# Token tiles in plain column order, and gather loads that read every fourth column

## The chip, the cores and the metric

The kernel runs on one core of one Trainium2 chip. The metric is device time in microseconds (us) of one execution; the median of three runs stands for the kernel, and lower is better. One execution was also profiled, and every row below comes from it.

## What is computed

Two transformer-like blocks run one after the other on 256 tokens of width 1024. The first has two layers of gated linear attention with spatial gating, cross attention and a mixture of experts; the second has block attention, a state space mixer, another mixture of experts and a gated projection. So there are three mixtures of experts (called 0, 1 and 2 below), and the change touches only these. Each has 16 experts with a hidden width of 512 and takes two experts for a token:

```python
for e in range(N_EXPERTS):
    h = jax.nn.silu(xt @ w_gate[e]) * (xt @ w_up[e])
    y = y + gate[:, e:e + 1] * (h @ w_down[e])
```

`gate` is zero but for the two experts that a token's router chose. Data are float32 all through.

## The kernel before, in words

**An expert works on its own tokens.** When no expert has more than 64 of the 256 tokens, each expert gets a tile of 64 columns that holds its tokens only, with the model's 1024 values in 8 chunks of 128 partitions (`own_even` for one quad of four experts, `own_odd` for the next). Moving the tokens into those columns is a matrix product, `gather` (line 966): the stationary operand is a 128 x 128 piece of `x_tok` (tokens on partitions, 128 model columns), and the moving operand is `picked` (tokens on partitions, 4 experts x 64 places, 256 columns), which has a one where a token takes a place. `x_tok` is a pair, a value rounded for the multiplier (`aux_high`) and the rest (`aux_low`), and there are two tiles of 128 tokens, so one chunk takes four matmuls, and one call of `gather`, for two chunks, takes eight, each with a load of its own.

**Where the gathers stand.** TensorE (PE) makes four calls for the first quad right after routing (`experts`, line 952; 32 matmuls). The other three quads are gathered inside the loop over experts of `experts_own` (line 1041), one call per expert for the first twelve experts, between the sum of an earlier expert's output (`add`, line 1103) and the up projection (`gate_up`, line 1055); that is 12 x 8 = 96 matmuls. ScalarE (ACT) then copies each result from PSUM into `own_even` or `own_odd` (`packed`, line 1507).

**Column order.** The expert weights come in by DMA with four consecutive rows on one partition (`"(p r) n -> p (r n)"` for each half of the matrix). So chunk c of the activations must hold, on partition p, the model column 512 (c // 4) + 4 p + (c % 4). Before the change the token tiles are stored in that order already: ScalarE's line 1569 (in `routing_input`) and VectorE's line 2005 (in `routing_input_low`) read plain columns and write each value 128 places after its neighbour, and `gather` then loads 128 adjacent columns.

**Order around routing.** ScalarE goes, for each of the two token tiles, through `tiles_high` (line 1454, the transposed activations for the router), line 1569, and line 1570 (the residual). VectorE (DVE) goes through `tiles_low` (line 1802) and line 2005 for each tile, and then the router's small steps, up to `choose` (line 1996), which makes `picked`. TensorE's router product (lines 935, 936, 940, 949) needs lines 1454 and 1802 of both tiles; the gathers need line 2005 of both and `picked`. SyncE's queue of weight loads waits for line 2005 once per mixture, before it lends `x_res` to the weights (line 415).

The branch for crowded experts (`experts_all`) also reads `x_tok`; the profiled execution has no row of it.

Of the kernel before, what the change touches and what calls it, by code (L numbers as in the profile page):

```python
# [18 lines left out]
F32 = mybir.dt.float32  # L19
F32R = mybir.dt.float32r  # L20
ACT = mybir.ActivationFunctionType
ALU = mybir.AluOpType
AX = mybir.AxisListType.X

P = 128
# [24 lines left out]
def build(nc, a, out):  # L50
    DEPTH, D = a["w_in"].shape[0], a["w_in"].shape[1]
    T = a["x"].shape[1]
# [92 lines left out]
    OWN = P // 2  # L145
    QUAD = 4
# [131 lines left out]
    with ExitStack() as ctx:  # L278
# [34 lines left out]
        ident = sb("ident", [P, P])  # L313
# [31 lines left out]
        S = {n: sem(n) for n in names}  # L345
# [144 lines left out]
        all_hid = own[1][:, 0:FC, :].rearrange("p c n -> p (c n)").rearrange("p (t n) -> p t n", t=TT)  # L490
        all_hidT = own[1][:, FC:2 * FC, :]

        def regrouped(v):

            return v.rearrange("q (i r p) -> q i p r", i=2, r=4)

        def runs(v):

            return v.rearrange("q (i p r) -> q i p r", i=2, r=4)

        x_tok = [v[:].rearrange("p c t -> p (c t)").rearrange("p (t n) -> p t n", t=TT) for v in (aux_high, aux_low)]
        gates = st[:, 512:512 + TT * NE].rearrange("p (t n) -> p t n", t=TT)
# [206 lines left out]
        def _(pe):  # L709
# [256 lines left out]
            def gather(m, q, g, dst):  # L966

                for c in range(2):
                    for part in range(2):
                        for t in range(TT):  # L970
                            c0 = (2 * g + c) * P
                            i = pe.matmul(dst[:, c * QUAD * OWN:(c + 1) * QUAD * OWN], x_tok[part][:, t, c0:c0 + P],  # L972
                                          picked[q % 2][:, t, :, 0, :], start=(part + t == 0), stop=(part + t == TT))
                i.then_inc(x_filled[m], 1)

# [13 lines left out]
            def experts_all(m):  # L989

                G, U, TS, Y0 = (ps[:, 2 * s:2 * s + 2, :] for s in (G_SLOT, U_SLOT, T_SLOT, Y0_SLOT))
                residual(m, start=False, stop=True)
                pe.wait_ge(x_packed[m], GROUPS)
                flat = ps[:, 0:4, :].rearrange("p b n -> p (b n)")
                for c in range(KC):
                    for t in range(TT):
                        for part in range(2):
                            i = pe.matmul(flat[:, c * T + t * P:c * T + t * P + P], x_tok[part][:, t, c * P:c * P + P].bitcast(F32), ident[:],
                                          start=(part == 0), stop=(part == 1))
                i.then_inc(tokens_turned[m], 1)  # L1000
                pe.wait_ge(tokens_copied[m], 2)

                def wide(e, part):
                    if e:
                        pe.wait_ge((silu_done, hid_ready)[part][m], e)
                    for j in range(2):
                        w = tile(m, (gate_at, up_at)[part](e) + j)
                        for r in range(4):
                            c = 4 * j + r
                            for t in range(TT):  # L1010
                                i = pe.matmul((G, U)[part][:, t, :], tok_T[:, c, t * P:t * P + P], w[:, FF * r:FF * r + FF], start=(c == 0), stop=(c == KC - 1))
                        i.then_inc(tiles_used, 1)

                for part in range(2):
                    wide(0, part)
                for e in range(NE):
                    pe.wait_ge(hid_ready[m], e + 1)
                    if e:
                        pe.wait_ge(y_added[m], TT * e)
                    dst = TS.rearrange("p b n -> p (b n)").rearrange("p (c t) -> p c t", t=T)  # L1020
                    by_run = all_hid.rearrange("p t (i s r) -> p t i r s", i=2, r=2)
                    for i2 in range(2):
                        for r in range(2):
                            for t in range(TT):
                                i = pe.transpose(dst[:, 2 * i2 + r, t * P:t * P + P], by_run[:, t, i2, r, :], ident[:])
                    i.then_inc(hid_turned[m], 1)
                    if e + 1 < NE:
                        for part in range(2):
                            wide(e + 1, part)
                    pe.wait_ge(hid_copied[m], e + 1)  # L1030
                    for j in range(2):
                        w = tile(m, down_at(e) + j)
                        for r in range(2):
                            for t in range(TT):
                                for b in range(2):
                                    i = pe.matmul((Y0, TS)[t][:, b, :], all_hidT[:, 2 * j + r, t * P:t * P + P], w[:, D * r + 512 * b:D * r + 512 * b + 512],
                                                  start=(j + r == 0), stop=(j + r == 2))
                        i.then_inc(tiles_used, 1)
                pe.wait_ge(y_added[m], TT * NE)
# [116 lines left out]
            for l in range(DEPTH):  # L1156
# [16 lines left out]
                for t in range(TT):  # L1173
                    i = pe.matmul(slot_ps(L + "z")[:, t * DQK:t * DQK + DQK], aT[:, t * P:t * P + P], w_a2, start=True, stop=True)
# [7 lines left out]
                for g in range(SG):  # L1182
                    i = pe.transpose(slot_ps(L + "wsT")[:, g * P:g * P + P], ws_raw[:, g, :], ident[:])
# [6 lines left out]
                for k in range(PAIRS):  # L1190
                    for t in range(TT):
                        i = pe.matmul(slot_banks(L + "decay")[:, 1, 4 * k + 2 * t:4 * k + 2 * t + 2], log_a[:, t, k * P:k * P + P], half[:], start=True, stop=True)
# [4 lines left out]
                for k in range(PAIRS):  # L1197
                    for t in range(TT):
                        i = pe.transpose(slot_ps(L + "qT")[:, k * T + t * P:k * T + t * P + P], qk[:, t, k * P:k * P + P], ident[:])
# [11 lines left out]
                for k in range(PAIRS):  # L1211
                    begin(L + f"kv{k}")
                    for c in range(NCH):
                        t, hf = c // 2, c % 2
                        rows = slice(LCH * hf, LCH * hf + LCH)
                        i = pe.matmul(slot_banks(L + f"kv{k}")[:, hf, 256 * t:256 * t + 256], k_dec[rows, t, k * P:k * P + P],
                                      v_gla[rows, t, k * 2 * DV:(k + 1) * 2 * DV], start=True, stop=True)
# [6 lines left out]
                for t in range(TT):  # L1224
                    for g in range(SG):
                        i = pe.matmul(slot_banks(L + "mix_sgu")[:, t, g * P:g * P + P], wsT[:, g, :], gelu_v[:, t, g * P:g * P + P], start=True, stop=True)
# [3 lines left out]
                for t in range(TT):  # L1230
                    begin(L + f"o{t}")
                    for k in range(PAIRS):
                        for par in range(2):
                            rows = slice(DK * par, DK * par + DK)
                            for hf in range(2):
                                c = 2 * t + hf
                                i = pe.matmul(slot_banks(L + f"o{t}")[LCH * hf:LCH * hf + LCH, par, k * P:k * P + P],
                                              qT_gla[rows, k, c * LCH:c * LCH + LCH], state[rows, k, c, :], start=True, stop=True)
# [24 lines left out]
                for t in range(TT):  # L1263
                    begin(L + f"pT{t}")
                    pe.wait_ge(S["p_ready"], TT * l + t + 1)
                    for h in range(XH):
                        for b in range(TT):
                            i = pe.transpose(slot_ps(L + f"pT{t}")[:, (2 * h + b) * P:(2 * h + b + 1) * P], prob[:, t, h, b * P:b * P + P], ident[:])
                    full(i, L + f"pT{t}")
                operand_ready(L + "pT0", L + "pT1", L + "xva", L + "xvb")  # L1270
                for k in range(2):
                    begin(L + f"oT{k}")
                    for f in range(4):
                        fb = 4 * k + f
                        for b in range(TT):
                            i = pe.matmul(slot_ps(L + f"oT{k}")[:, f * T:f * T + T], xv[:, b, fb * P:fb * P + P], pT[:, fb // 2, b, :],
                                          start=(b == 0), stop=(b == TT - 1))
# [145 lines left out]
        def _(act):  # L1423
            chain = Counter(act, S["act_chain"])
            n, limit = 0, moe_at[0][0]
            A = nc.scalar.activation
# [138 lines left out]
            def routing_input(names, src, scale):  # L1565

                for t in range(TT):
                    tiles_high(act_high, names[t:t + 1], t)
                    A(regrouped(x_tok[0][:, t, :]), runs(src[:, t, :]), ACT.Copy).then_inc(S["tok_high"], 1)
                    A(y_acc[:, t, :], x[:, t, :], ACT.Copy, scale=scale).then_inc(S["residual_ready"], 1)  # L1570

            for l in range(DEPTH):
# [55 lines left out]
                for t in range(TT):  # L1628
                    act.wait_ge(S["smax_ready"], TT * l + t + 1)
                    for h in range(XH):  # L1630
                        i = A(prob[:, t, h, :], slot_ps(L + f"s{t}")[:, h * T:h * T + T], ACT.Exp, bias=neg_max[:, t, h:h + 1],
                              scale=float(XD) ** -0.5, accum_out=p_sum[:, t, h:h + 1])
# [92 lines left out]
            for t in range(TT):  # L1725
                act.wait_ge(S["u_ready"], t + 1)
                for g in range(SGR):
                    i = A(usq[:, t, g * 512:g * 512 + 512], zs[:, t, g * 512:g * 512 + 512], ACT.Square, accum_out=u_ms[:, t, g:g + 1])
# [39 lines left out]
        def _(dve):  # L1768
            V = nc.vector
# [159 lines left out]
            flat = lambda v: v.rearrange("p t g e -> p t (g e)")  # L1929
# [70 lines left out]
            def routing_input_low(names, src, m):  # L2000

                for t in range(TT):
                    tiles_low(act_low, act_high, names[t:t + 1], t)
                    dve.wait_ge(S["tok_high"], TT * m + t + 1)
                    V.tensor_tensor(regrouped(x_tok[1][:, t, :]), runs(src[:, t, :]), regrouped(x_tok[0][:, t, :]).bitcast(F32), ALU.subtract).then_inc(S["tok_low"], 1)

            def experts(m):

# [92 lines left out]
            for l in range(DEPTH):  # L2101
# [28 lines left out]
                for t in range(TT):  # L2130
                    for g in range(SG):
                        i = V.bn_stats(v_bn[:, t, g, :], gelu_v[:, t, g * P:g * P + P])
                link(i)
                for t in range(TT):
                    for g in range(SG):
                        i = V.bn_aggr(v_mv[:, t, g, :], v_bn[:, t, g, :])
# [3 lines left out]
                for t in range(TT):  # L2140
                    for g in range(SG):
                        at = slice(g * P, g * P + P)
                        i = V.scalar_tensor_tensor(gelu_v[:, t, at], gelu_v[:, t, at], v_mv[:, t, g, 0:1], sln_g[:, at], ALU.subtract, ALU.mult)
# [291 lines left out]
```

## Time and profile before

| | us |
|---|---|
| median of the three runs | 1481.27 |
| lowest and highest run | 1480.82, 1482.7 |
| the profiled execution's own time | 1480.01 |
| its span, first to last instruction | 1478.3 |
| TensorE busy in the span | 1396.9 |
| VectorE, ScalarE busy | 607.5, 498.2 |

The mean granted TensorE clock is 0.982 of full speed. The span is 1.7 us shorter than the same execution's own time. Matmuls overlap their neighbours: the duration of one is its way through the array, and the distance between two starts (called the pitch below) is what one costs in a stream. "PEld" is the load of a stationary operand, which overlaps the matmul ahead of it.

### The profile page before, as it was taken

To read this page: it belongs to the slowest core of one execution; us is meant where nothing else is said; L and a number is where in the kernel's file an instruction comes from. 1 tells how busy PE (TensorE), PEld (TensorE's weight loads), DVE (VectorE), ACT (ScalarE), POOL (GpSimd) and SP (SyncE) were. 2 spreads that over 40 slices of the span, in tenths; PEclk is the share of its full clock that TensorE was granted. 3 is DMA by queue.
4 is the path that set the end of the run, shared out by engine and by line. 5 is a ranking of instruction groups with operands and counts; after the bars stand their busy time and mean duration, and the time that the engine had idled before them with its cause. 6 is when DMAs were issued, how large, how long until landed. Compare 5 with 4: busy or idle time off the path is not lost.

```text
span 1478.3 us, 20927 instructions
## 1 busy us (share of the span) xinstructions
PE 1396.9 (94%) x8927; PEld 1000.5 (68%) x8927; DVE 607.5 (41%) x1001; ACT 498.2 (34%) x695; POOL 53.8 (4%) x95
## 2 busy tenths in 40 slices
PE   7999998999997999998999999799999989999977
PEld 5788976555554788986655554788787765555546
DVE  4677435111114585646111111657766561111124
ACT  5454434111113544443211111466565331111123
POOL 5000000000001000000000000000000000000000
PEclk9999999999999999999999999999999999999989
DMA  9556458999999455647899999453443769999970
GB/s 326 198 166 205 148 212 327 423 421 421 421 420 343 139 170 171 206 168 311 331 420 421 421 420 410 172 171 115 142 143 129 280 248 412 421 421 420 421 294 29
DMA packets 90807, 422.71 MB, mean 286 GB/s; under 512 B 7068, under 2 KB 7232, under 8 KB 53840
## 3 DMA queue, kind: packets, MB, share of 16 engines
q1 hardware_dynamic: 86528, 407.92, 70.8%
q0 software_dynamic: 4176, 13.30, 2.6%
q8 instruction: 78, 1.28, 0.4%
q14 instruction: 25, 0.20, 0.0%
HBM read 420.15 MB, written 1.05 MB: 285 GB/s over the span
## 4 chain that ended last, share of the span: by engine, by line
PE 88%; DVE 5%; ACT 4%; issue 2%; POOL 0%; DMA 0%; DVEq 0%; POOLq 0%; ACTq 0%
PE ps L1055 23%; PE ps L1091 12%; PE ps L753 5%; PE ps L754 5%; PE ps L758 5%; PE ps L972 4%; PE ps L1103 4%; PE ps L867 3%; PE ps L801 3%; PE ps L874 3%; PE ps L868 3%; PE ps L802 3%; PE ps L806 3%; PE ps L1080 1%; PE ps L914 1%
## 5 line engine op out<-in xcount | busy, mean ns | idle before, releaser
L1782 DVE TENSOR_TENSOR raw_low<-raw,w_high 128x1024 fp32r<-128x1024 f32 x198 | 237.4, 1223 | 171.2 <-ACT w_high L1440 170.5
L1440 ACT ACTIVATE w_high<-raw 128x1024 fp32r<-128x1024 f32 x198 | 206.6, 1058 | 258.6 <-PE ps L758 115.2
L2067 DVE TENSOR_TENSOR hid<-silu_g,ps 128x256 f32<-128x256 f32 x48 | 29.6, 616 | 259.8 <-PE ps L1055 259.8
L753 PE MATMUL ps<-w_high,act_high 128*128 128x512 f32 x272 | 110.6, 407 | 6.4 <-DVE raw_low L1782 3.6
L2075 DVE SCALAR_TENSOR_TENSOR out_low<-ps,stats,out_high 128x512 fp32r<-128x512 f32 x48 | 36.1, 751 | 182.3 <-ACT out_high L1546 182.3
L754 PE MATMUL ps<-raw_low,act_high 128*128 128x512 f32 x272 | 108.4, 399 | 0.0
L758 PE MATMUL ps<-w_high,act_low 128*128 128x512 f32 x272 | 103.3, 393 | 0.0
L1055 PE MATMUL ps<-raw,own_odd 128*64 128x256 f32 x800 | 91.6, 380 | 0.0
L1546 ACT ACTIVATE out_high<-ps,stats 128x512 fp32r<-128x512 f32 x48 | 33.0, 687 | 161.5 <-PE ps L1091 161.5
L867 PE MATMUL ps<-act_high,w_high 128*128 128x256 f32 x288 | 81.7, 287 | 5.4 <-issue 3.4
L1541 ACT ACTIVATE spread<-ps 128x288 fp32r<-128x288 f32 x48 | 19.7, 411 | 186.7 <-PE ps L1080 186.7
L1055 PEld LDWEIGHTS ps<-raw,own_odd 128*64 128x64 f32 x800 | 56.6, 137 | 36.8 <-issue 11.0
L868 PE MATMUL ps<-act_high,raw_low 128*128 128x256 f32 x288 | 81.2, 285 | 0.0
L874 PE MATMUL ps<-act_low,w_high 128*128 128x256 f32 x288 | 78.4, 285 | 0.0
L1091 PE MATMUL ps<-raw,hT 128*64 128x512 f32 x328 | 76.2, 599 | 0.0
L801 PE MATMUL ps<-w_high,act_high 128*128 128x512 f32 x192 | 75.2, 392 | 0.0
L802 PE MATMUL ps<-raw_low,act_high 128*128 128x512 f32 x192 | 74.8, 389 | 0.0
L1055 PE MATMUL ps<-raw,own_even 128*64 128x256 f32 x640 | 74.6, 382 | 0.0
L753 PEld LDWEIGHTS ps<-w_high,act_high 128*128 128x128 f32 x272 | 52.7, 194 | 20.9 <-issue 6.8
L659 POOL TENSOR_TENSOR stats<-stats,exponent 128x1 f32<-128x1 f32 (+2 forms) x24 | 19.9, 830 | 1217.7 <-DVE stats L1851 302.1
L1537 ACT ACTIVATE silu_g<-ps 128x256 f32<-128x256 f32 x48 | 18.4, 384 | 130.7 <-PE ps L1055 130.7
L2071 DVE COPY hT<-ps 128x256 f32<-128x256 f32 x48 | 20.4, 425 | 102.1 <-PE ps L1067 102.1
(411 smaller groups left out, 2570.8 us busy)
## 6 DMA issues: line engine op xcount, KB each, us to landing
raw<-in_w_up SPq DMA_DIRECT2D x46, 1024.0 KB, 11.3
raw<-in_w_in SPq DMA_DIRECT2D x44, 1024.0 KB, 9.2
raw<-in_w_gate SPq DMA_DIRECT2D x44, 1024.0 KB, 13.1
raw<-in_w_down SPq DMA_DIRECT2D x41, 1024.0 KB, 16.7
work<-in_w_down SPq DMA_DIRECT2D x23, 1024.0 KB, 19.7
work<-in_w_gate SPq DMA_DIRECT2D x21, 1024.0 KB, 7.9
w_lent<-in_w_gate SPq DMA_DIRECT2D x18, 1024.0 KB, 13.0
w_lent<-in_w_down SPq DMA_DIRECT2D x14, 1024.0 KB, 14.8
```

Source lines behind the costliest of these rows:

```text
L753: pe.matmul(bank[:, t, :], xh, wh, start=(k == 0), stop=False)
L754: pe.matmul(bank[:, t, :], xh, wl, start=False, stop=False)
L758: return pe.matmul(bank[:, t, :], src[1][:, k, t * P:t * P + P], weights(n, 512 * c, 512 * c + 512)[0], start=False, stop=(k == KC - 1))
L801: pe.matmul(slot_banks(names[t])[:, b, :], xh, wh, start=(k == 0), stop=False)
L802: pe.matmul(slot_banks(names[t])[:, b, :], xh, wl, start=False, stop=False)
L867: pe.matmul(bank, wh, src[0][:, k, 0:T], start=(k == 0), stop=False)
L868: pe.matmul(bank, wl, src[0][:, k, 0:T], start=False, stop=False)
L874: return pe.matmul(bank, wh, src[1][:, k, 0:T], start=False, stop=(k == KC - 1))
L1055: i = pe.matmul((G, U)[part][OWN * h:OWN * h + OWN, 0:256], own[e // QUAD % 2][:, c, OWN * (e % QUAD):OWN * (e % QUAD) + OWN], w[:, FF * r ...
L1091: i = pe.matmul(Y[OWN * h:OWN * h + OWN, :], hT[:, r, OWN * j:OWN * j + OWN], w[:, D * r + 512 * h:D * r + 512 * h + 512], start=(j + r == ...
L1440: A(split_unit(n)[0], raw_unit(n), ACT.Copy).then_inc(high_ready, 1)
L1782: V.tensor_tensor(split_unit(n)[1], raw_unit(n), split_unit(n)[0].bitcast(F32), ALU.subtract).then_inc(low_ready, 1)
```

## The change

The token tiles are now written in plain column order, by both engines. The gather picks its columns itself: chunk c is read as columns 512 (c // 4) + (c % 4), and then every fourth one, 128 in all, so two neighbours in the stationary operand lie 16 bytes apart in memory. The number, the shapes and the order of the instructions are the same on every engine; only the way in which two kinds of store and two kinds of load step through memory differs.

```diff
@@ -490,13 +490,9 @@
         all_hid = own[1][:, 0:FC, :].rearrange("p c n -> p (c n)").rearrange("p (t n) -> p t n", t=TT)
         all_hidT = own[1][:, FC:2 * FC, :]
 
-        def regrouped(v):
-
-            return v.rearrange("q (i r p) -> q i p r", i=2, r=4)
-
-        def runs(v):
-
-            return v.rearrange("q (i p r) -> q i p r", i=2, r=4)
+        def columns_of(v, c):
+
+            return v.rearrange("q (i p r) -> q i r p", i=2, r=4)[:, c // 4, c % 4, :]
 
         x_tok = [v[:].rearrange("p c t -> p (c t)").rearrange("p (t n) -> p t n", t=TT) for v in (aux_high, aux_low)]
         gates = st[:, 512:512 + TT * NE].rearrange("p (t n) -> p t n", t=TT)
@@ -968,8 +964,7 @@
                 for c in range(2):
                     for part in range(2):
                         for t in range(TT):
-                            c0 = (2 * g + c) * P
-                            i = pe.matmul(dst[:, c * QUAD * OWN:(c + 1) * QUAD * OWN], x_tok[part][:, t, c0:c0 + P],
+                            i = pe.matmul(dst[:, c * QUAD * OWN:(c + 1) * QUAD * OWN], columns_of(x_tok[part][:, t, :], 2 * g + c),
                                           picked[q % 2][:, t, :, 0, :], start=(part + t == 0), stop=(part + t == TT))
                 i.then_inc(x_filled[m], 1)
 
@@ -995,7 +990,7 @@
                 for c in range(KC):
                     for t in range(TT):
                         for part in range(2):
-                            i = pe.matmul(flat[:, c * T + t * P:c * T + t * P + P], x_tok[part][:, t, c * P:c * P + P].bitcast(F32), ident[:],
+                            i = pe.matmul(flat[:, c * T + t * P:c * T + t * P + P], columns_of(x_tok[part][:, t, :], c).bitcast(F32), ident[:],
                                           start=(part == 0), stop=(part == 1))
                 i.then_inc(tokens_turned[m], 1)
                 pe.wait_ge(tokens_copied[m], 2)
@@ -1566,7 +1561,7 @@
 
                 for t in range(TT):
                     tiles_high(act_high, names[t:t + 1], t)
-                    A(regrouped(x_tok[0][:, t, :]), runs(src[:, t, :]), ACT.Copy).then_inc(S["tok_high"], 1)
+                    A(x_tok[0][:, t, :], src[:, t, :], ACT.Copy).then_inc(S["tok_high"], 1)
                     A(y_acc[:, t, :], x[:, t, :], ACT.Copy, scale=scale).then_inc(S["residual_ready"], 1)
 
             for l in range(DEPTH):
@@ -2002,7 +1997,7 @@
                 for t in range(TT):
                     tiles_low(act_low, act_high, names[t:t + 1], t)
                     dve.wait_ge(S["tok_high"], TT * m + t + 1)
-                    V.tensor_tensor(regrouped(x_tok[1][:, t, :]), runs(src[:, t, :]), regrouped(x_tok[0][:, t, :]).bitcast(F32), ALU.subtract).then_inc(S["tok_low"], 1)
+                    V.tensor_tensor(x_tok[1][:, t, :], src[:, t, :], x_tok[0][:, t, :].bitcast(F32), ALU.subtract).then_inc(S["tok_low"], 1)
 
             def experts(m):
 
```

## Rows read from the trace of the kernel before

**Rows 1.** Page: span, busy share of each engine; then time granted and DMA in three mixtures

```profile
span 1478.3 us, 20927 instructions
PE 1396.9 (94%) x8927; PEld 1000.5 (68%) x8927; DVE 607.5 (41%) x1001; ACT 498.2 (34%) x695; POOL 53.8 (4%) x95
...
core 0: us, PE busy (x) PEld busy (x) DVE busy (x) ACT busy (x) POOL busy (x), PEclk, DMA share, GB/s
240.00:470.00 230.00, 221.20 (x1600) 125.04 (x1600) 41.71 (x90) 40.80 (x74) 0.56 (x1) 0.99 0.99 403
```

**Rows 2.** Chain of waits, one expert of mixture 0: start us, us, what

```profile
300.05 1.15 PE ps L972 x8
301.20 3.60 PE ps L1055 x32
304.81 0.46 PE ps L1080 x2
305.26 3.58 PE ps L1091 x16
308.85 3.45 PE ps L1055 x32
312.30 0.37 PE ps L1067 x2
312.67 1.12 PE ps L1103 x8
313.79 1.14 PE ps L972 x8
```

**Rows 3.** Waits of PE and of SyncE's queue: us in total, times, longest us

```profile
PE ps L972 <- DVE picked_even L1996: 5.8, 3, 1.9
...
PE ps L914 <- DMA x_res<-in_x: 4.6, 1, 4.6
...
SPq L597 <- PE ps L1055: 404.0, 175, 14.4
...
SPq L415 <- DVE aux_low L2005: 15.0, 2, 9.3
```

**Rows 4.** The gather's line alone, by stretch: opening and loop of each mixture (PE, PEld)

```profile
240.00:247.00 7.00, 5.56 (x32) 5.38 (x32) 0.76 0.47 193
247.00:430.00 183.00, 14.56 (x96) 12.12 (x96) 1.00 1.00 412
...
701.00:708.00 7.00, 5.55 (x32) 5.38 (x32) 0.76 0.51 215
...
1209.00:1213.30 4.30, 4.06 (x32) 3.89 (x32) 1.00 0.01 4
1213.30:1400.00 186.70, 14.57 (x96) 12.13 (x96) 1.00 1.00 411
```

**Rows 5.** The gather's line: duration ns min/median/max; then its timeline, low and full clock

```profile
L972 PEld LDWEIGHTS ps<-picked_even,aux_high x96: 186/189/336, 240.7 to 1308.8; 128*128 128x128 f32 x96
...
242.33 0.63 PE L972 MATMUL ps<-picked_even,aux_high 128*128 128x256 f32 x2
242.76 0.63 PE L972 MATMUL ps<-picked_even,aux_low 128*128 128x256 f32 x2
...
300.56 0.40 PE L972 MATMUL ps<-picked_even,aux_high 128*128 128x256 f32 x2
300.80 0.40 PE L972 MATMUL ps<-picked_even,aux_low 128*128 128x256 f32 x2
```

**Rows 6.** Timeline: six loads of 128 columns with matmuls of 16 columns

```profile
237.49 0.74 PEld L1146 LDWEIGHTS ps<-stats,tri 128*128 128x128 f32 x6 [1.48 <-issue]
```

**Rows 7.** ACT and DVE, stores out of order and plain: duration ns min/median/max

```profile
L1569 ACT ACTIVATE aux_high<-x_res x4: 2019/2092/2188, 225.6 to 690.5; 128x1024 fp32r<-128x1024 f32 x4
...
L1570 ACT ACTIVATE work<-x_res x6: 1057/1064/1141, 227.4 to 1198.9; 128x1024 f32<-128x1024 f32 x6
...
L2005 DVE TENSOR_TENSOR aux_low<-x_res,aux_high x4: 1985/2014/2083, 228.0 to 692.7; 128x1024 fp32r<-128x1024 f32 x4
...
L1782 DVE TENSOR_TENSOR raw_low<-raw,w_high x198: 1214/1225/1228, 10.5 to 1454.4; 128x1024 fp32r<-128x1024 f32 x198
```

**Rows 8.** Timeline around routing, mixture 0, and VectorE's first router step of mixture 2

```profile
227.01 1.09 PE L914 MATMUL ps<-ident,x_res 128*128 128x128 f32 x8 [0.68 <-DVE x_res L1840]
...
228.33 1.02 ACT L1454 ACTIVATE act_high<-ps 128x1024 fp32r<-128x1024 f32 x1
...
231.42 1.99 DVE L2005 TENSOR_TENSOR aux_low<-x_res,aux_high 128x1024 fp32r<-128x1024 f32 x1 [0.23 <-ACT aux_high L1569]
...
232.95 0.26 PE L949 MATMUL ps<-ident,own_even 16*128 16x16 f32 x2 [0.55 <-ACT own_even L1459]
...
233.32 0.18 DVE L1936 TENSOR_TENSOR stats<-ps,bias 128x32 f32<-128x32 f32 x1
...
1202.64 0.19 DVE L1955 TENSOR_TENSOR stats<-ps,bias 128x32 f32<-128x32 f32 x1 [1.55 <-PE ps L949]
```

## The prediction

> **What bounds the kernel.** I began with the page: TensorE is busy 94% of the span, VectorE 41% and ScalarE 34% [rows 1], so first look at whether TensorE is also what ends last. The chain of waits says so for the part that the change touches: in the loop over experts its pieces follow one another without a gap, all of them on TensorE, and the gather (line 972) is one of them, 8 matmuls in 1.15 us out of a round of some 13.7 us (300.05 to 313.79) [rows 2]. DMA is just as full there (0.99 of its share) [rows 1], so the next view was the waits, to see who waits for whom. TensorE's only wait for a DMA in the whole run is the one for the input; SyncE's queue, on the other hand, waits 404.0 us in 175 waits for line 1055 to give back weight buffers [rows 3]. The weights are ahead of TensorE, not behind. So **a longer gather is paid in full** in the loop: nothing in the round has slack to take it up, and a slower TensorE only makes the weights come earlier by comparison.
>
> **Part 1, the loads (added cost).** There are 3 x 96 = 288 gather matmuls in the loops and 3 x 32 = 96 in the openings, 384 in all (the middle mixture's loop repeats the first's) [rows 4]. Each moves 256 columns and needs one load of 128 columns. At the full clock four matmuls in a row start 0.24 us a pair apart, a pitch of about 0.119 us [rows 5]. How near is the load to being the limit? Line 1146 answers that: six loads of 128 columns with matmuls of only 16 columns take 0.74 us, and one takes 0.19, so loads follow one another every (0.74 - 0.19) / 5 = 0.110 us [rows 6]. **The load has 0.119 - 0.110 = 0.009 us of slack**; whatever it grows beyond that sets the pitch.
>
> No row of this trace has a stationary operand with a step between its columns, so the price must be bounded. Below: nothing, if the load reads with a step as fast as without. Above: from the operations that do step through memory. ScalarE's out-of-order copy takes 2092 ns for 1024 values where the plain one takes 1064; VectorE's out-of-order subtraction takes 2014 ns where the plain one takes 1225 [rows 7]. That is 1.00 and 0.77 ns more for each value. Two engines with different rates of their own (1064 and 1225 ns) get nearly the same surcharge and end at nearly the same time, which looks like a limit of the memory and not of the engine, and the load goes to the same memory. For 128 columns it gives 0.099 to 0.128 us a load, less the slack 0.090 to 0.119, and I take the middle, **0.105 us a load**. The steps differ (512 bytes in those stores, 16 bytes in this load) and those are writes and this is a read; both can make the truth smaller, down to nothing, and that is the main rival below. I don't choose the lower end because the load, at 0.110 us / 128 = 0.86 ns a column, already asks for its values faster than the plain forms of those two engines do (1.04 and 1.20 ns a value), so it should be no better than they are at hiding a slow access.
>
> - Loops: 288 x 0.105 = **+30.2 us** (bounds 0 and 288 x 0.119 = 34.3).
> - Openings at the full clock: the windows show clock 0.76 in the 7 us of each of the first two openings and 1.00 in the third [rows 4]. In the low stretch of about 3 us a pair starts 0.43 us after the last, a pitch of 0.213 to 0.215 [rows 5], so some 14 of 32 matmuls of each of the first two openings run there. That leaves 96 - 28 = 68: 68 x 0.105 = **+7.1 us**.
> - Openings at the low clock: 28 matmuls. Their pitch of 0.214 is already about what a stepped load would need (0.110 + 0.114 = 0.224), if the surcharge is the memory's: 28 x 0.01 = **+0.3 us**. If it instead counts in TensorE's cycles it doubles with everything else, 28 x 0.21 = 6 us; I keep that for the upper end.
>
> The Trainium skill bears on this at one point. Advanced Engine Details and Errata, section Memory Cachelines, says that SBUF has 16-byte lines, that at least two accesses must hit a line to absorb the memory's latency, and that a different line at each access costs a penalty. By it a load of every fourth float32 column takes a new line each time and is charged, as I forecast; it gives no size, so the sum stays with the rows. SBUF — State Buffer, in the section on the DMA port swizzle, adds that a step is free up to "4 fp32", which is exactly this step; read so, the term is nothing and the time is that of the first rival.
>
> **Part 2, the stores (saved time).** Lines 1569 and 2005 come 6 times each. With plain stores I expect 1.06 and 1.22 us in place of 2.1 and 2.0 [rows 7], 1.0 and 0.8 us less each, 11 us of engine time in all. Hardly any of it is on the path. In mixture 0 ScalarE starts line 1454 of the second tile at 228.33, though TensorE's transposes ended at 227.01 + 1.09 = 228.10: with a shorter line 1569 it starts some 0.2 us sooner. VectorE's first router step starts at 233.32 behind line 2005, which began at 231.42; it could start at 233.24, just after line 949 ends at 232.95 + 0.26 = 233.21 [rows 8]. Together 0.2 + 0.1 = 0.3 us. Mixture 1 has the same pattern, **-0.3 us** again. In mixture 2 VectorE sits idle 1.55 us for line 949 before that step [rows 8], so there nothing is gained. Sum **-0.6 us**. What then sets the start of the gathers is the router's chain as before: line 972 waits for `picked`, not for the token tiles, 1.9 us each time [rows 3]. SyncE's loads that wait for line 2005 (15.0 us in 2 waits [rows 3]) are let go some 2 us sooner; as TensorE never waits for them, that is worth nothing, and if that cover were gone it would be worth at most these 2 us a mixture.
>
> **Sum.** +30.2 + 7.1 + 0.3 - 0.6 = +37.0 us on the profiled execution's 1480.0, that is 1517. This execution is 1.3 us below the median of the runs, well inside what I don't know, so I leave the number at **1517 us**. The case's own range: 356 full-clock loads x 0.090 = 32.0, less 0.6, gives 1511; 356 x 0.119 = 42.4 plus 6, less 0.6, gives 1528.
>
> **Rivals.**
> 1. *A stepped load costs nothing* (the other side, not slower). The mechanism: only stores pay for stepping, since a store that covers a part of what the memory handles at once has to be done by itself, and the load brings in its column ahead of the matmul. For it: every row that shows the surcharge is a store; no row shows a stepped read that is slow. Against it: the slack of 0.009 us is thin, so the load's surcharge must be under 9 ns in 110, some 8%, for this to hold. Then only part 2 is left, and the time is 1479.4, **no measurable change** against a median of 1481.3 (some 0.2%, or 3 us, is what a measurement can tell from no change here). Chance 0.30.
> 2. *A part of the surcharge*. A read pays half of what a store pays, 0.4 to 0.5 ns a column: 0.057 us a load, less the slack 0.048, 356 x 0.048 = 17, less 0.6: **1496**. Nothing in the trace speaks for a half in particular. Chance 0.10.
> 3. *The clock falls as well.* With loads twice as long the array idles half the time in an opening, where the granted clock is already down for some 3 us in two of three mixtures [rows 4]. If all 32 matmuls of each opening ran at the low clock and the load doubled there too (0.43 us each), an opening would take 13.7 us in place of 5.6, 5.6 and 4.1: +25.8 in all. With the loops 1480.0 + 30.2 + 25.8 - 0.6 = **1535**. For it: the low stretches stand behind TensorE's idle time in routing. Against it: the third opening shows 1.00 all through after just such idle time. Chance 0.05.
>
> **The numbers.** The forecast has 0.55, the rivals 0.30, 0.10 and 0.05. Slower by over 0.2%: 0.55 + 0.10 + 0.05 = 0.70. The first rival is nearly all within 0.2%; I give 0.02 of it to a gain of over 0.2%, if the earlier start of routing shortens a stretch at the low clock: same 0.28, faster 0.02. The likeliest case's own range is 1511 to 1528. For 8 in 10 the range must reach down to the first rival and needs no more than the upper part of the forecast: 1479 to 1526.
>
> **What would show it.** Right: the loads of line 972 last 290 ns or so in place of 189, 8 gathers of a round take about 2.0 us in place of 1.15 in the chain, with the other pieces of the round as they were; lines 1569 and 2005 near 1.06 and 1.2 us; VectorE's first router step some 0.3 us nearer to the transposes in mixtures 0 and 1. Wrong: loads still at 189 ns and a gather of 1.15 us (first rival); a load in between (second); granted clock below 1 through the openings, the third one's too (third). The prediction is also wrong if a round of the loop stays at 13.7 us although the gather is longer, since then TensorE had slack that the chain does not show.

## The result, and the profile after

The changed kernel takes 1519.5 us (median of 4 runs, 1518.0 to 1521.5), the kernel before 1482.0 us in the same comparison: ratio 1.0257, 95% interval 1.024 to 1.0273, so 2.6% slower, some 36 to 40 us. The forecast was 1517 us, in a range of 1479 to 1526.

| profiled execution | before | after |
|---|---|---|
| own time, us | 1480.01 | 1517.95 |
| span, us | 1478.3 | 1516.1 |
| TensorE busy, us | 1396.9 | 1437.4 |
| VectorE, ScalarE busy, us | 607.5, 498.2 | 602.6, 493.0 |
| mean granted TensorE clock | 0.982 | 0.983 |

The page of the changed kernel, span and busy shares (beside [rows 1]):

```profile
span 1516.1 us, 20927 instructions
PE 1437.4 (95%) x8927; PEld 1041.0 (69%) x8927; DVE 602.6 (40%) x1001; ACT 493.0 (33%) x695; POOL 53.7 (4%) x95
```

TensorE's busy time and its loads' both grow by 40.5 us; the other two engines lose 5 us each, about what the shorter stores save (below). The number of instructions is the same. The gather's line is now 967, the up projection 1050, the sum 1098, the down projection 1086. Its rows, duration in ns min/median/max (beside [rows 5]):

```profile
L967 PEld LDWEIGHTS ps<-picked_even,aux_high x96: 307/330/339, 240.1 to 1343.8; 128*128 128x128 f32 x96
L967 PE MATMUL ps<-picked_even,aux_high x96: 374/399/513, 240.1 to 1344.0; 128*128 128x256 f32 x96
```

The load went from 189 to 330 ns. In the chain of waits the same round of the loop (start us, us, what; beside [rows 2]) now reads:

```profile
305.43 2.08 PE ps L967 x8
307.50 3.60 PE ps L1050 x32
311.11 0.46 PE ps L1075 x2
311.57 3.58 PE ps L1086 x16
315.15 3.45 PE ps L1050 x32
318.61 0.37 PE ps L1062 x2
318.98 1.13 PE ps L1098 x8
320.10 2.10 PE ps L967 x8
```

Every other piece has the length it had, to 0.01 us. Only the gather grew, from 1.15 to 2.08 us, and the next one starts after 14.67 us (320.10) in place of 13.74. Nothing in the round took any of it up. The gather's line alone by stretch, opening and loop of mixture 0 and openings of mixtures 1 and 2 (PE and PEld busy, granted clock, DMA share, GB/s; beside [rows 4]):

```profile
240.00:248.50 8.50, 7.76 (x32) 7.59 (x32) 0.80 0.34 142
248.50:440.00 191.50, 25.85 (x96) 23.50 (x96) 1.00 1.00 410
714.00:722.00 8.00, 7.76 (x32) 7.59 (x32) 0.79 0.36 151
1233.00:1241.07 8.07, 7.68 (x32) 7.58 (x32) 0.79 0.09 38
```

The timeline of the first opening holds something more: each row is a pair of matmuls, the first four are from its stretch at the low clock, the last two from its stretch at the full clock. The two windows' rows behind it give the clock (0.50, then 1.00; the row's columns are those of [rows 1]):

```profile
241.64 0.68 PE L967 MATMUL ps<-picked_even,aux_low 128*128 128x256 f32 x2
242.11 0.68 PE L967 MATMUL ps<-picked_even,aux_high 128*128 128x256 f32 x2
242.59 0.67 PE L967 MATMUL ps<-picked_even,aux_low 128*128 128x256 f32 x2
...
244.00 0.67 PE L967 MATMUL ps<-picked_even,aux_high 128*128 128x256 f32 x2
...
244.89 0.63 PE L967 MATMUL ps<-picked_even,aux_high 128*128 128x256 f32 x2
...
247.23 0.63 PE L967 MATMUL ps<-picked_even,aux_low 128*128 128x256 f32 x2
```

```profile
241.70:244.20 2.50, 2.50 (x12) 2.50 (x12) 1.13 (x4) 0.60 (x1) 0.00 (x0) 0.50 0.47 193
245.20:247.50 2.30, 2.30 (x12) 2.30 (x11) 0.00 (x0) 0.60 (x1) 0.00 (x0) 1.00 0.00 0
```

At half the clock five pairs take 2.36 us (241.64 to 244.00), at the full clock 2.34 (244.89 to 247.23): a pair starts every 0.47 us in both. **The stepped load takes its 0.235 us whatever clock TensorE is granted**, where the pitch of before went from 0.119 to 0.214 [rows 5].

The stores (medians beside [rows 7]):

```profile
L1564 ACT ACTIVATE aux_high<-x_res x4: 1043/1048/1051, 225.1 to 702.7; 128x1024 fp32r<-128x1024 f32 x4
...
L2000 DVE TENSOR_TENSOR aux_low<-x_res,aux_high x4: 1214/1216/1218, 227.6 to 704.0; 128x1024 fp32r<-128x1024 f32 x4
```

and what stands behind them at the end of mixture 0's router product (beside [rows 8]):

```profile
227.72 1.02 ACT L1449 ACTIVATE act_high<-ps 128x1024 fp32r<-128x1024 f32 x1 [0.58 <-PE ps L910]
...
232.71 0.19 DVE L1931 TENSOR_TENSOR stats<-ps,bias 128x32 f32<-128x32 f32 x1 [1.57 <-PE ps L945]
```

At both places the engine now waits for TensorE (`<-PE`), where before it came late.

### The profile page after: what moved, and what is told of

Its sections match the earlier page's. It is cut to its first block, busy times and chain, and to the rows that moved or that the text cites. A ratio compares the mean times of both kernels' runs of the same rounds, so it can differ in the third digit from the quotient of the medians.

```text
span 1516.1 us, 20927 instructions
## 1 busy us (share of the span) xinstructions
PE 1437.4 (95%) x8927; PEld 1041.0 (69%) x8927; DVE 602.6 (40%) x1001; ACT 493.0 (33%) x695; POOL 53.7 (4%) x95
## 4 chain that ended last, share of the span: by engine, by line
PE 89%; DVE 5%; ACT 3%; issue 2%; POOL 0%; DMA 0%; DVEq 0%; POOLq 0%; ACTq 0%
PE ps L1050 22%; PE ps L1086 11%; PE ps L967 6%; PE ps L749 5%; PE ps L750 5%; PE ps L754 5%; PE ps L1098 4%; PE ps L863 3%; PE ps L864 3%; PE ps L870 3%; PE ps L797 3%; PE ps L798 3%; PE ps L802 3%; PE ps L910 1%; PE ps L1075 1%
## 5 line engine op out<-in xcount | busy, mean ns | idle before, releaser
L1050 PEld LDWEIGHTS ps<-raw,own_even 128*64 128x64 f32 x640 | 44.3, 137 | 25.9 <-issue 4.2
```

Of the source, the lines that this page charges most:

```text
L1050: i = pe.matmul((G, U)[part][OWN * h:OWN * h + OWN, 0:256], own[e // QUAD % 2][:, c, OWN * (e % QUAD):OWN * (e % QUAD) + OWN], w[:, FF * r ...
```

## The experiments

The first two take the change apart. In them the chunks hold other model columns than the expert weights expect.

**Stores alone** (the stores of the change, the loads of before):

```diff
-i = pe.matmul(dst[...], columns_of(x_tok[part][:, t, :], 2 * g + c),
+i = pe.matmul(dst[...], x_tok[part][:, t, (2 * g + c) * P:(2 * g + c) * P + P],
```

> The plain stores of the change with the adjacent loads of the kernel before (the chunks then hold other model columns than the expert weights expect; nothing else is changed). Theory 'load': the stepped load is the whole slowdown, so this is level with the kernel before, some 0.5 us faster at most (ratio 1.000); ScalarE's copy 1.05 us, VectorE's subtraction 1.22 us, gather of 8 matmuls 1.15 us. Rival 'timing': the slowdown comes from routing that ends earlier and meets other work or the clock at another moment: then this run is slower too, by 1% or more.

Measured: 1479.8 us against 1481.6, ratio 0.999 (0.9975 to 1.0006). The two stores take 1047 and 1216 ns, the gather 1.15 us. So the stores slow nothing; a gain as small as the one worked out can't be told from none by time.

**Loads alone** (the loads of the change, the stores of before):

```diff
-i = pe.matmul(dst[...], x_tok[part][:, t, c0:c0 + P],
+i = pe.matmul(dst[...], columns_of(x_tok[part][:, t, :], 2 * g + c),
```

> The stores of the kernel before with the stepped loads of the change (again other columns than the weights expect). Theory 'load': +38 us, ratio 1.025 to 1.027, a gather of 8 matmuls 2.08 us in the chain, load 330 ns. Rival 'timing': level with the kernel before.

Measured: 1522.5 us against 1481.6 (+40.8 us, a little over the +38 expected), ratio 1.0274 (1.0252 to 1.0296); the load 330 ns, the gather 2.08 us. The whole slowdown is in the 384 loads. "Timing" falls.

**What in the step costs.** Three kernels change the step alone. Every third column (wrong columns for the weights):

```diff
-return v.rearrange("q (i p r) -> q i r p", i=2, r=4)[:, c // 4, c % 4, :]
+return v[:, 90 * c:90 * c + 3 * P].rearrange("q (p r) -> q r p", r=3)[:, 0, :]
```

> The change with loads that read every third column (12 bytes apart) in place of every fourth; the columns are not those that the weights expect. Theory 'groups': what costs is leaving a group of four neighbouring values (16 bytes), 1.83 ns each; 128 columns at step 3 touch 96 groups, so a pitch of 96 x 1.83 = 0.176 us and about +19 us over the kernel before. Rival 'threshold': any step under 16 bytes is free and a step of 16 is charged in full: pitch 0.119, level with the kernel before. Rival 'any step': only adjacent columns are fast: pitch 0.235, +38 us.

Measured: 1497.6 us, ratio 1.0113 (1.0089 to 1.0136), some 16 to 17 us over before and short of the +19 expected, though the pitch fits; a gap of that size between the pitch and the medians comes up again in "The sum". The timeline of one gather from its second pair on:

```profile
302.41 0.51 PE L967 MATMUL ps<-picked_even,aux_low 128*128 128x256 f32 x2
302.75 0.51 PE L967 MATMUL ps<-picked_even,aux_high 128*128 128x256 f32 x2
303.10 0.52 PE L967 MATMUL ps<-picked_even,aux_low 128*128 128x256 f32 x2
```

Pairs start 0.34 to 0.35 us apart, a pitch of 0.173: what "groups" gave (0.176), and neither 0.119 nor 0.235. "Threshold" and "any step" fall.

Every eighth column (the stores interleave all eight chunks in runs of four; in this cut and the next the helpers' expressions are written out in place):

```diff
-A(x_tok[0][:, t, :], src[:, t, :], ACT.Copy)
+A(x_tok[0][:, t, :].rearrange("q (p i r) -> q i p r", i=2, r=4), src[:, t, :].rearrange("q (i p r) -> q i p r", i=2, r=4), ACT.Copy)
-return v.rearrange("q (i p r) -> q i r p", i=2, r=4)[:, c // 4, c % 4, :]
+return v.rearrange("q (p c) -> q c p", c=KC)[:, c, :]
```

(VectorE's line likewise.)

> The change with a token tile in which the eight chunks are interleaved: the stores write runs of four neighbours, the loads read every eighth column (32 bytes apart); it computes the same. Theory 'groups': the load costs the same as at step 4 (128 groups either way), pitch 0.235 us, +38 us. Rival 'distance': the price grows with the step, pitch over 0.25 us. The stores in runs of four show whether a store is free when it fills a group: near 1.05 and 1.22 us by 'groups', near 2.0 us if any break in the order costs.

Measured: 1521.0 us, ratio 1.0272 (1.0248 to 1.0297); the load 337 ns, pairs 0.48 us apart, the gather 2.13 us: twice the distance costs 2% more a load. The stores that write runs of four take 1048 and 1216 ns, as fast as plain ones. "Distance" falls.

Pairs: the stores write two neighbours at a time, the loads read every second column.

```diff
-A(x_tok[0][:, t, :], src[:, t, :], ACT.Copy)
+A(x_tok[0][:, t, :].rearrange("q (s y r) -> q y s r", s=2, r=2), src[:, t, :].rearrange("q (y s r) -> q y s r", s=2, r=2), ACT.Copy)
-return v.rearrange("q (i p r) -> q i r p", i=2, r=4)[:, c // 4, c % 4, :]
+return v.rearrange("q (s i p r) -> q s i r p", s=2, i=2, r=2)[:, c % 4 // 2, c // 4, c % 2, :]
```

> A middle way that computes the same: the stores write pairs of neighbours (8 bytes) and the loads read every second column. Theory 'groups': a load of 128 columns touches 64 groups, 64 x 1.83 = 0.117 us, so the pitch stays near 0.12 and the time level with the kernel before (within 2 us); the stores touch a new group for every pair, 512 x 1.83 = 0.94 us plus 0.2, so they are near their plain 1.05 and 1.22 us. Rival 'any step': loads 330 ns, pitch 0.235, +38 us.

Measured: 1482.2 us against 1481.5, ratio 1.0008 (0.9995 to 1.0021). Load and stores:

```profile
L975 PEld LDWEIGHTS ps<-picked_even,aux_high x96: 193/195/334, 240.4 to 1308.9; 128*128 128x128 f32 x96
...
L1572 ACT ACTIVATE aux_high<-x_res x4: 1132/1139/1146, 225.6 to 690.3; 128x1024 fp32r<-128x1024 f32 x4
...
L2008 DVE TENSOR_TENSOR aux_low<-x_res,aux_high x4: 1214/1218/1218, 228.0 to 691.6; 128x1024 fp32r<-128x1024 f32 x4
```

The load is 6 ns longer than with adjacent columns, inside the prediction's 9 ns of slack; VectorE pays nothing and ScalarE 0.09 us, near the 0.94 + 0.2 of the expectation. It computes the same and is level with the kernel before; it gains nothing that can be measured. Pairs that lie across the border of two groups were not run, and neither were reads in pairs by ScalarE or VectorE.

**Are reads of the other engines charged too?** Before, the stores jumped and the reads were plain. Here it is the other way round, with the same result in memory:

```diff
-return v.rearrange("q (i r p) -> q i p r", i=2, r=4)
+return v.rearrange("q (i r p) -> q i r p", i=2, r=4)
-return v.rearrange("q (i p r) -> q i p r", i=2, r=4)
+return v.rearrange("q (i p r) -> q i r p", i=2, r=4)
```

> Kernel before, but ScalarE and VectorE walk the tile in the order of the destination: they write plain and read every fourth value of their source; it computes the same and the gather loads adjacent columns. Theory 'groups' holds for any read: the two operations cost about 2.0 us each as before, time level with the kernel before. Rival 'stores and loads only': reads of ScalarE and VectorE are free to step, 1.05 and 1.22 us, and the time is up to 0.6 us below the kernel before, the best version.

Measured: 1481.5 us, ratio 0.9995 (0.9984 to 1.0007):

```profile
L1569 ACT ACTIVATE aux_high<-x_res x4: 2060/2072/2095, 229.0 to 693.5; 128x1024 fp32r<-128x1024 f32 x4
...
L2005 DVE TENSOR_TENSOR aux_low<-x_res,aux_high x4: 1989/1994/2002, 231.5 to 695.6; 128x1024 fp32r<-128x1024 f32 x4
```

A read is charged as a store is (2092 and 2014 ns [rows 7]). The first rival's reason, that only stores pay, is wrong in general and not only for this load.

**And TensorE's moving operand?** The gather with adjacent loads, and every fourth column of the token tile as its moving operand in place of the selection matrix:

```diff
-picked[q % 2][:, t, :, 0, :], start=(part + t == 0), stop=(part + t == TT))
+x_tok[part][:, t, :].rearrange("q (p r) -> q r p", r=4)[:, 0, :], start=(part + t == 0), stop=(part + t == TT))
```

> The gather with adjacent loads, but with a moving operand of 256 columns that reads every fourth column of the token tile in place of the selection matrix, so the expert tiles hold products of tokens (only mixture 0 is compared, and only the gather's rows). Theory 'groups': 256 x 1.83 = 0.468 us a matmul, 8 of them 3.8 us in place of 1.15. Rival: TensorE's moving read is not charged and the pitch stays 0.119.

Measured, in mixture 0:

```profile
307.63 0.65 PE L972 MATMUL ps<-aux_low 128*128 128x256 f32 x2
308.09 0.65 PE L972 MATMUL ps<-aux_high 128*128 128x256 f32 x2
308.56 0.65 PE L972 MATMUL ps<-aux_low 128*128 128x256 f32 x2
```

Neither expectation holds. The step is charged, but with half of what "groups" said: 0.233 us a matmul of 256 columns, 0.91 ns a column, where the load pays 0.235 / 128 = 1.83. So the price of a group is not one number for all of TensorE. One way to join the two is that a float32 load reads its columns twice. The transposes test it, since they also load 128 float32 columns, in less time:

```diff
-i = pe.transpose(dst[:, c, :], src[:, t, c * P:c * P + P], ident[:])
+i = pe.transpose(dst[:, c, :], src[:, t, :].rearrange("q (i p r) -> q i r p", i=2, r=4)[:, c // 4, c % 4, :], ident[:])
```

(The features come out in another order, which the computation after them does not expect.)

> Kernel before, but the 128 x 128 transposes of token tiles (line 914) load every fourth column, so the features come out in another order; only the transposes' rows are compared. Their load of adjacent columns is short (140 ns, a pitch of 0.107 us with a matmul of 128 columns). The moving operand at step 4 was charged 0.9 ns a column, the load of a gather 1.83 ns. Theory 'double read': a value that leaves the group costs 0.9 ns on TensorE and a float32 load reads its columns twice, a transpose's load once: load about 140 + 128 x (0.90 - 0.42) = 200 ns. Rival 'load port': any load is charged 1.83 ns a column: 140 + 128 x (1.83 - 0.42) = 320 ns.

Measured:

```profile
L914 PEld LDWEIGHTS ps<-ident,x_res x112: 195/212/226, 4.5 to 1444.6; 128*128 128x128 f32 x112
...
228.34 1.03 PEld L914 LDWEIGHTS ps<-ident,x_res 128*128 128x128 f32 x8 [0.95 <-DVE x_res L1840]
```

212 ns, near the 200 of "double read" and far from 320. The second row says it more directly: eight loads take 1.03 us and one takes 0.21, so they follow one another every 0.82 / 7 = 0.117 us, which is 0.91 ns a column, the price of the moving operand and half that of the gather's load. The rows fit the theory; they don't show the two readings themselves.

**What else moved between the profiles.** The two kernels were profiled once more, unaltered:

> The changed kernel unaltered, for a second profile: which of the differences outside the gathers (clock in the router's product of mixture 2, the last 45 us) repeat. Theory 'phase': they come from the moments at which the granted clock falls and rises and differ from profile to profile by 1 us or so at each place; the gathers repeat to 0.1 us (7.7 us an opening, 2.08 us a call). Rival: the gains of 1.6 us in mixture 2's routing and 1.4 us at the end belong to the change and repeat.

> The kernel before unaltered, for a second profile. Theory 'phase': the spans outside the gathers scatter by about 1 us a place between two profiles of one kernel, above all in mixture 2's routing (20.75 us from the root to the first gather in the first profile of before, 19.19 us in that of after) and after the last expert (47.6 and 46.1 us). Rival: both repeat to 0.2 us and belong to the change.

Their single times are 1520.2 and 1482.0 us. With these, and the kernels above that leave the rest alone, one can cut each profile at the same events: "routing" from the first inverse square root (on POOL) of the norm ahead of the router to the first gather, "mixture" from the first gather to the start of the last expert's last sum, "end" from there to the end of the span. "Rest" is what the span has beyond these, in which no kernel of the table differs from another. In us, for mixtures 0, 1, 2:

| kernel | routing | mixture | end | rest | span |
|---|---|---|---|---|---|
| before | 20.43, 20.48, 20.75 | 223.00, 223.00, 221.51 | 47.56 | 701.6 | 1478.3 |
| before again | 20.43, 21.84, 19.24 | 223.02, 223.01, 223.01 | 45.86 | 703.9 | 1480.3 |
| loads alone | 20.43, 20.44, 19.25 | 236.59, 236.60, 236.58 | 46.18 | 705.0 | 1521.1 |
| stores alone | 20.18, 20.24, 19.15 | 223.84, 223.01, 223.00 | 45.86 | 702.4 | 1477.7 |
| after | 20.25, 20.16, 19.19 | 236.59, 236.60, 236.58 | 46.13 | 700.6 | 1516.1 |
| after again | 20.17, 20.17, 19.21 | 236.65, 236.66, 236.62 | 46.60 | 702.3 | 1518.4 |

Three things can be read off it. A mixture costs 13.6 us more with stepped loads than the 223.0 us of most mixtures without, and 15.1 more than the short one of 221.5. Plain stores shorten the routing of mixtures 0 and 1 by 0.2 to 0.3 us each and that of mixture 2 by less than 0.1. And 1 to 2 us come and go at other places with no change of code: in the opening of a mixture (223.0 or 221.5), in a routing (20.75 or 19.24, 21.84 or 20.48), at the end, and over 4 us in the rest. So the 1.6 us of mixture 2's routing and the 1.4 us at the end between the first two profiles can't be credited to the change. The granted clock goes with them. Here are routings as windows, 20.75 us of "before", 21.84 and 19.24 of "before again" (columns as in [rows 1]):

```profile
1188.48:1209.23 20.75, 15.35 (x78) 10.60 (x77) 17.10 (x41) 8.98 (x12) 1.70 (x3) 0.92 0.93 376
...
683.95:705.79 21.84, 16.53 (x83) 11.21 (x82) 17.31 (x39) 10.21 (x15) 2.20 (x4) 0.92 1.01 409
1192.19:1211.43 19.24, 13.83 (x78) 9.69 (x77) 17.08 (x41) 9.00 (x12) 1.70 (x3) 1.00 0.99 401
```

The long ones ran at a mean clock of 0.92, the short one at 1.00; and the opening of 221.51 is the one whose gathers ran at the full clock [rows 4]. Whole runs show it as well: of the 23 runs of the kernel before that stand beside the pairs and the stepped reads, the four with a mean clock of 0.977 took 1483.5 to 1485.9 us and the four with 0.983 took 1477.8 to 1480.4. "Phase" holds.

## Why the prediction was right

**The bound.** That a longer gather is paid in full rested on a chain without gaps and on a DMA queue that waits for TensorE. It held to the hundredth: the round grew by the gather's 0.93 us and no more (13.74 to 14.67).

**Part 1, loops.** Forecast +0.105 us a load and +30.2 us. Measured pitch 0.235 against 0.119, +0.116 us; the windows' rows give 25.85 - 14.57 = 11.3 us a loop, 33.8 in all. The term was 0.011 us a load too small, a tenth: I took the middle of 0.090 and 0.119 where the truth lay near ScalarE's end. The step that was wrong is that it carried a surcharge over, when the surcharge depends on how fast each engine is without it; what carries over is the time per visit. ScalarE shows it without TensorE: its stores of 1024 single values take 2078 ns in "loads alone" and those of 512 pairs 1139 ns, so (2078 - 1139) / 512 = 1.83 ns a visit, and 128 x 1.83 = 0.234 us is the measured pitch of the load.

**Part 1, openings.** Forecast 7.4 us. Measured 7.76 - 5.56 = 2.2 us in mixtures 0 and 1 and 7.68 - 4.06 = 3.6 in mixture 2 (its baseline was the short one), 8.0 in all; beside the 223.0 of the other mixtures (whose openings took 5.56) the third would be 2.1, 6.5 in all. That the forecast lies between is partly luck: it took the one opening at the full clock for a property of mixture 2, and in "before again" that opening has the low clock like the others (mean 0.80, mixture 223.01 us). The reading that the surcharge is the memory's and not the clock's was right: 0.47 us a pair at either clock. Of the third rival's condition a part came true: the mean clock was 0.79 to 0.80 in all three openings, low in a part of each and not in all 32 matmuls. Its price did not come at all, since a load that takes 0.235 us at either clock loses nothing by the lower one.

**Part 2.** Forecast -0.3, -0.3 and 0; measured -0.2 to -0.3 twice and under 0.1. The place was right as well: ScalarE's second line 1449 now waits for the transposes and VectorE's first router step for line 945.

**The sum.** The mixtures give 3 x 13.6 = 40.8 us and routing -0.5, so +40.3, against +37.0 forecast; the medians differ by 37.5, and the interval (1.024 to 1.0273) reaches from 35.6 to 40.5. The forecast is closer to the medians than its terms are to theirs: that +37.0 lies so near to 37.5 is in part luck. The table says where the difference went in the profiles. In the first pair the span grew by 37.8 us: +42.3 in the mixtures, -2.1 in routing (1.6 of it mixture 2's), -1.4 at the end and -0.9 in the rest; in the second pair by 38.1: +40.9, -2.0, +0.7 and -1.6. Whether these gains outside the mixtures are scatter of the clock or an effect of the changed code on where the low stretches fall is open: "loads alone", which lacks the plain stores, measured +40.8 us, and "stores alone" 1.8 us under before with an interval that reaches from a gain of 3.7 us to a loss of 0.9.

**The rivals.** The first fell in its mechanism, by the stepped reads of ScalarE and VectorE. The second, a part of the surcharge, is what the moving operand shows, but not the load. The rule of the Trainium skill that spoke for the forecast (Advanced Engine Details and Errata, section Memory Cachelines: at least two hits on a 16-byte line) agrees with the runs: two values of a line per visit cost next to nothing (6 ns on a load at step 2, 0.09 us on ScalarE's stores in pairs), one is charged, runs of four are free. The Trainium skill's other wording (SBUF — State Buffer, in the section on the DMA port swizzle: free up to "4 fp32") does not agree: a step of exactly 4 costs the full price, and a step of 3 already half of it.

## What to carry to other kernels

Count how many groups of 16 bytes an access pattern visits, and charge each visit 1.83 ns on ScalarE, on VectorE and in an ordinary float32 load of TensorE: the operation takes that (on ScalarE 0.2 us more) or its usual time, whichever is longer. A transpose's load and a moving operand paid half. The runs had 4-byte values only, at steps of 1, 2, 3, 4 and 8 columns and as pairs and runs of four. So a reordering of float32 values was as good as free where each visit to a group used two of them (stores in pairs, a load at step 2), and a jump that must be made belongs on an engine with idle time (here 6 stores of each of two engines, 0.5 us on the path) and not in an operand that TensorE loads 384 times (40 us). To see whether a longer instruction will be paid, look at the chain around it for pieces without gaps, then at who waits for whom.

## What the runs showed that was not expected

- The price counts in time, not in the engine's cycles: 0.235 us a load at TensorE's clock of 0.50 and of 1.00, and 1.83 ns a value for engines whose plain forms take 1064 and 1225 ns for the same 1024 values.
- TensorE's moving operand pays half of that: 0.91 ns a column at step 4. A transpose's load at step 4 takes 212 ns where an ordinary float32 load takes 330 (140 and 189 ns with adjacent columns); its pitch is 0.117 us against 0.235.
- Stores in pairs cost ScalarE 1139 ns (512 x 1.83 ns + 0.2 us) and VectorE nothing (1218 ns), which fits with VectorE's own rate for a pair: 1218 / 512 = 2.4 ns, slower than 1.83.
- With such loads the mixtures are steadier: all nine in three profiles take 236.6 to 236.7 us, while those with adjacent loads take 221.5 to 223.8, with the clock in the opening. The runs as a whole are not: the rest scatters as before.
